# Two transformer blocks on one core: the sandwich norms of the first block taken in two halves of the tokens

## The reference

```python
for l in range(DEPTH):
    h = rms_norm(x, attn_pre_g[l])
    proj = h @ w_in[l]
    ...
    x = x + rms_norm(mixed @ w_out[l], attn_post_g[l])
    h = rms_norm(x, ffn_pre_g[l])
    y = (jax.nn.silu(h @ w_gate[l]) * (h @ w_up[l])) @ w_down[l]
    x = x + rms_norm(y, ffn_post_g[l])
```

## Time and profile before

| | |
|---|---|
| median of 3 runs (lowest to highest) | 2709.44 us (2707.68 to 2710.03) |
| the profiled execution, its own time | 2704.35 us |
| its span, first to last instruction | 2702.6 us |
| TensorE clock granted, share of full | 0.985 |
| PE matmuls busy | 2606.3 us (96%) |
| DVE busy | 1651.4 us (61%) |
| ACT busy | 748.6 us (28%) |
| POOL busy | 456.5 us (17%) |

### The profile page before, as it was taken

How to read it: one execution, slowest core, us unless ns; L and a number is a source line. 1 busy time by engine, 2 the same in 40 slices (tenths; PEclk the granted TensorE clock), 3 DMA queues, 4 the chain that set the end, 5 groups by cost and what they waited for, 6 DMA issues and landing times.

```text
span 2702.6 us, 38398 instructions
## 1 busy us (share of the span) xinstructions
PE 2606.3 (96%) x12250; PEld 2058.9 (76%) x12250; DVE 1651.4 (61%) x2625; ACT 748.6 (28%) x1391; POOL 456.5 (17%) x454
## 2 busy tenths in 40 slices
PE   8999899999899989999899989999999999999999
PEld 5776688887577668888766658888888887788887
DVE  6754666454775566645567776544458888564452
ACT  3333232120333333212145541100025555210000
POOL 4111111112111111212201101111211111112111
PEclk9999999999899999999989999999999999999999
DMA  3221233333122123333312113333332221233333
GB/s 110 55 63 53 76 90 100 94 97 99 48 62 63 55 70 98 96 94 101 93 40 63 54 32 93 101 94 95 99 94 63 63 62 47 78 94 101 93 101 94
DMA packets 417270, 214.80 MB, mean 79 GB/s; under 512 B 6819, under 2 KB 416014, under 8 KB 417166
## 3 DMA queue, kind: packets, MB, share of 16 engines
q1 hardware_dynamic: 416144, 212.89, 27.3%
q10 hardware_dynamic: 1022, 0.58, 0.1%
HBM read 211.34 MB, written 2.10 MB: 79 GB/s over the span
## 4 chain that ended last, share of the span: by engine, by line
PE 84%; DVE 7%; ACT 4%; issue 3%; POOL 1%; DVEq 0%; ACTq 0%; POOLq 0%
PE acc L633 71%; PE sc L740 2%; PE sc L1051 1%; PE tp L633 1%; PE tp L763 1%; PE po L786 1%; PE po L633 1%; ACT scratch L1916 1%; ACT scratch L1914 1%; DVE scratch L1440 1%; PE aux L646 1%; PE tp L902 1%; DVE xT L1359 1%; DVE w_lo L1170 1%; PE po L773 0%
## 5 line engine op out<-in xcount | busy, mean ns | idle before, releaser
L633 PE MATMUL acc<-h_hi,w_hi 128*128 128x512 f32 x1968 | 811.0, 412 | 31.0 <-DVE h_lo L1148 24.4
L576 POOL TENSOR_SCALAR w_hi<-w_raw 128x1024 fp32r<-128x1024 f32 x390 | 418.7, 1074 | 2200.4 <-PE acc L633 2130.3
L633 PE MATMUL acc<-h_lo,w_hi 128*128 128x512 f32 x1968 | 775.0, 394 | 0.0
L633 PE MATMUL acc<-h_hi,w_lo 128*128 128x512 f32 x1968 | 775.0, 394 | 0.0
L1170 DVE TENSOR_TENSOR w_lo<-w_raw,w_hi 128x1024 fp32r<-128x1024 f32 x390 | 477.6, 1225 | 76.3 <-POOL w_hi L576 76.2
L633 PEld LDWEIGHTS acc<-h_hi,w_hi 128*128 128x128 f32 x1968 | 373.2, 190 | 142.6 <-issue 40.4
L633 PE MATMUL acc<-mid_hi,w_hi 128*128 128x512 f32 x1120 | 440.4, 393 | 7.3 <-DVE mid_lo L1701 3.2
L633 PE MATMUL acc<-mid_lo,w_hi 128*128 128x512 f32 x1120 | 440.0, 393 | 0.0
L633 PE MATMUL acc<-mid_hi,w_lo 128*128 128x512 f32 x1120 | 438.2, 391 | 0.0
L633 PEld LDWEIGHTS acc<-h_lo,w_hi 128*128 128x128 f32 x1968 | 373.8, 190 | 80.5 <-issue 10.6
L633 PEld LDWEIGHTS acc<-h_hi,w_lo 128*128 128x128 f32 x1968 | 372.8, 189 | 81.6 <-issue 1.4
(11 more groups left out here) (316 smaller groups left out, 2665.1 us busy)
## 6 DMA issues: line engine op xcount, KB each, us to landing
w_raw<-in_mlp_w_dram SPq DMA_DIRECT2D x128, 512.0 KB, 4.1
w_raw<-in_w_in_dram SPq DMA_DIRECT2D x48, 512.0 KB, 3.9
w_raw<-in_w_gate_dram SPq DMA_DIRECT2D x44, 512.0 KB, 3.7
w_raw<-in_w_up_dram SPq DMA_DIRECT2D x44, 512.0 KB, 3.7
w_raw<-in_w_down_dram SPq DMA_DIRECT2D x32, 512.0 KB, 4.1
w_raw<-in_hg_w_in_dram SPq DMA_DIRECT2D x32, 512.0 KB, 4.0
w_raw<-in_sb_w_qkv_dram SPq DMA_DIRECT2D x24, 512.0 KB, 3.8
w_raw<-in_w_out_dram SPq DMA_DIRECT2D x16, 512.0 KB, 4.1
```

The lines of the kernel that those rows point to most:

```text
L576: nc.gpsimd.tensor_scalar(to, w_raw[:, slot], 1.0, 1.0, ALU.mult, ALU.mult).then_inc(w_rounded, 1)
L633: mm = pe.matmul(bank[:], w[:, k], r[:, k], start=(k == 0 and i == 0), stop=(k == k_tiles - 1 and i == 2))
```

## The change

The 512 tokens are two halves of 256 columns. The last pair of output units is computed half by half (`last_pair`): both units for the first half, then both for the second; the squares of the first half are summed while the second half is multiplied. `normed_update` and `both_norms` scale, update x and form `h_hi` and `h_lo` for the first half of all eight tiles, and then for the second. `side_by_side` runs its units, too, once for each half, each matmul with 256 columns. The first two units now use the extra weight buffers and the other two the main ones, the PSUM banks change accordingly, and the order of the lags is turned round in the second half. The first norm (ahead of the loop) is done in halves with the same functions. The diff, cut:

```diff
-LAGS = [0, 0, 3, 4]
+FIRST_LAGS = [0, 0, 2, 3]
+SECOND_LAGS = [2, 3, 0, 0]
+HALF = S // 2
...
+            round_extra(0)
             for slot in range(2):
-                round_unit(0, slot, w_hi[:, slot], None)
-            round_extra(1)
+                round_unit(1, slot, w_hi[:, slot], None)
...
-                round_units(half + 2, U_GU0 // 2 - 1)
-                round_extra(half + U_GU0 // 2 + 1)
+                round_units(half + 2, U_GU0 // 2 - 2)
+                round_extra(half + U_GU0 // 2)
+                for slot in range(2):
+                    round_unit(half + U_GU0 // 2 + 1, slot, w_hi[:, slot], 2 * half + U_GU0 + slot + 1)
...
+            def sum_half(added, h):
+
+                pe.wait_ge(square_added, added)
+                pe.matmul(aux[:, columns(h)], ones[:, 0:P], square_sum[:, columns(h)], start=True,
+                          stop=True).then_inc(aux_done, 1)
...
+            def last_pair(half, hi, lo, k_tiles, added, a_n, taken):
+
+
+                def of(i, h):
+                    def before(k):
+                        if k == 0 and h == 0:
+                            pe.wait_ge(w_split, 2 * half + i + 3)
+                            pe.wait_ge(evacuated[i], half)
+                        if k == 0 and h == 1:
+                            pe.wait_ge(half_taken, taken + i + 1)
+                    return products(acc[i], hi, lo, w_hi[:, i], w_lo[:, i], k_tiles, unit_done if h else half_done, before,
+                                    columns(h))
+                run(of(0, 0))
+                run(of(1, 0))
+                ops = of(0, 1)
+                run(ops[:14])
+                pe.wait_ge(aux_free, a_n)
+                sum_half(added + KD, 0)
+                run(ops[14:])
+                run(of(1, 1))
+                pe.wait_ge(aux_free, a_n + 1)
...
-            def side_by_side(half, base, n, banks):
-
-                units = [unit(half, i, h_hi, h_lo, ready=h_ready, base=base, fresh=True) for i in range(2)]
-                units += [extra_unit(half + 1, i, bank, base) for i, bank in enumerate(banks)]
-                for k in range(KD + LAGS[len(units) - 1]):
-                    if k in (2, 4, 6, KD - 1):
-                        sum_pair(n * (KD // 2), (k - 1) // 2 if k < KD - 1 else KD // 2 - 1)
-                    for ops, lag in zip(units, LAGS):
-                        if 0 <= k - lag < KD:
-                            run(ops[3 * (k - lag):3 * (k - lag) + 3])
+            def side_by_side(half, norm, banks, added, a_n):
+
+
+                def of(n, h):
+                    def before(k):
+                        if k == 0 and h == 0:
+                            pe.wait_ge(w_split, 2 * half + n + 3)
+                        pe.wait_ge(h_ready, 2 * KD * norm + KD * h + k + 1)
+                    high, low = ((ex_hi, ex_lo) if n < 2 else (w_hi, w_lo))
+                    return products(banks[n], h_hi, h_lo, high[:, n % 2], low[:, n % 2], KD,
+                                    unit_done if h else None, before, columns(h))
+
+                count = len(banks)
+                for h, lags in ((0, FIRST_LAGS), (1, SECOND_LAGS)):
+                    units = [of(n, h) for n in range(count)]
+                    for k in range(KD + max(lags[:count])):
+                        if h == 0 and k == 3:
+                            sum_half(added, 1)
+                        for q, at in enumerate((5, 6, 7, 9) if h == 0 else (3, 4, 6, 7)):
+                            if k == at:
+                                if q == 0:
+                                    pe.wait_ge(aux_free, a_n + h)
+                                sum_pair(norm, h, q)
+                        for n in ((0, 1, 2, 3) if h == 0 else (2, 3, 0, 1)):
+                            if n < count and 0 <= k - lags[n] < KD:
+                                run(units[n][3 * (k - lags[n]):3 * (k - lags[n]) + 3])
...
-                        side_by_side(half0, l * 16, 2 * l, (po, tp[1]))
+                        side_by_side(half0, 2 * l, (sc[0], sc[1], po, tp[1]), added_base(2 * l), A + 1)
...
-                sum_squares(added_base(2 * l), A + AUX["norm_att_post"])
+                last_pair(half0 + U_OUT // 2 + KD // 2 - 1, mid_hi[:, 0], mid_lo[:, 0], KD, added_base(2 * l),
+                          A + AUX["att_post_a"], 4 * l)
...
-                            side_by_side(half, l * 16 + 8, 2 * l + 1, (po, sc[1]))
+                            side_by_side(half, 2 * l + 1, (sc[0], tp[0], po, sc[1]), added_base(2 * l + 1),
+                                         A + AUX["ffn_a"])
...
-                        side_by_side(U_SB // 2, block2_norm(0)[0], 2 * LAYERS, (tp[1],))
-                        work = extra_unit(U_SB // 2 + 1, 1, po, block2_norm(0)[0])
+                        side_by_side(U_SB // 2, 2 * LAYERS, (sc[0], sc[1], tp[1]), added_base(2 * LAYERS), A_SB + 1)
+                        work = products(po, h_hi, h_lo, w_hi[:, 1], w_lo[:, 1], KD, unit_done,
+                                        lambda k: pe.wait_ge(w_split, U_SB + 6) if k == 0 else None)
...
-            v.sem_inc(square_added, 2)
-
-            for j in range(KD):
-                low_part(0, j, gains[:, G_ATT_PRE + j:G_ATT_PRE + j + 1])
-                if j == 0:
-                    split_low(0, 0)
-                    split_low(0, 1)
-                if j % 2:
-                    add_pair(0, 0, j)
-                if j in (4, 6):
-                    split_extra(1, j // 2 - 2)
+            v.memset(square_sum[:, columns(1)], 0.0).then_inc(square_added, 1)
+            v.sem_inc(square_added, 1)
+
+            for h in range(2):
+                for j in range(KD):
+                    low_half(0, h, j, gains[:, G_ATT_PRE + j:G_ATT_PRE + j + 1])
+                    if h == 0 and j == 0:
+                        split_extra(0, 0)
+                        split_extra(0, 1)
+                    if h == 1 and j == 1:
+                        v.wait_ge(aux_done, 1)
+                    if j % 2:
+                        add_pair(KD * h + j + 1, 0, h, j)
+                    if h == 0 and j in (2, 4):
+                        split_low(1, j // 2 - 1)
...
+                def take_half(half, slot, h, n, first):
+
+                    if h == 0:
+                        v.wait_ge(half_done, 2 * n + slot + 1)
+                    else:
+                        take(half, slot)
+                    dst = yT[:, KD - 2 + slot, columns(h)]
+                    done = evacuated[slot] if h else half_taken
+                    if first:
+                        COPY(dst, acc[slot][:, columns(h)]).then_inc(done, 1)
+                    else:
+                        TT(dst, dst, acc[slot][:, columns(h)], ALU.add).then_inc(done, 1)
+
+                def add_half(n, h, slot, before):
+
+                    v.wait_ge(square_ready, squares_base(n) + KD - 2 + (1, 2, 3, 7)[2 * h + slot])
+                    v.wait_ge(square_added, added_base(n) + KD - 2 + before)
+                    s = square_sum[:, columns(h)]
+                    TT(s, s, post_square[slot][:, columns(h)], ALU.add).then_inc(square_added, 1)
+
+                def normed_update(g, n, half, following, first):
+
+                    take_half(half, 0, 0, n, first)
+                    split_extra(following, 0)
+                    add_half(n, 0, 0, 0)
+                    take_half(half, 1, 0, n, first)
+                    add_half(n, 0, 1, 1)
+                    split_extra(following, 1)
+                    take_half(half, 0, 1, n, first)
+                    add_half(n, 1, 0, 2)
+                    norm = n + 1
+                    squares = squares_base(n) + KD - 2
+                    for h in range(2):
+                        c = columns(h)
+                        v.wait_ge(rstd_ready, l * 8 + 2 * g + 3 + h)
+                        for j in range(KD + 1):
+                            if j < KD:
+                                STT(yT[:, j, c], yT[:, j, c], layer_gain[:, g, j:j + 1], rstd[:, c], ALU.mult,
+                                    ALU.mult).then_inc(y_scaled, 1)
+                            if j >= 1:
+                                low_half(norm, h, j - 1, layer_gain[:, g + 1, j - 1:j])
+                                if j % 2 == 0:
+                                    add_pair(squares + (4 + j + KD * h if j > 2 or h else 5), norm, h, j - 1)
+                            if j < KD:
+                                v.wait_ge(y_scaled, 2 * KD * n + KD * h + j + 1)
+                                TT(xT[:, j, c], xT[:, j, c], yT[:, j, c], ALU.add).then_inc(x_ready, 1)
+                            if h == 0 and j == 2:
+                                take_half(half, 1, 1, n, first)
+                                split_low(following + 1, 0)
+                            if h == 0 and j == 3:
+                                add_half(n, 1, 1, 3)
+                            if h == 0 and j == 4:
```

(42 more changed lines are left out.)

161 lines of the change are left out of this document (73 added, 88 removed).

## The result

| | before | after |
|---|---|---|
| median of the runs (lowest to highest) | 2709.74 us (2707.68 to 2711.05) | 2728.31 us (2727.98 to 2732.3) |
| ratio, 95% interval | | 1.0078 [1.0066, 1.009] |
| span of the profiled execution | 2702.6 us | 2730.6 us |

The change makes the kernel slower by 18.6 us, 0.78%. The forecast had the sign and a third of the size: +5.8 us, with a range that ended at 2725. The two profiled spans are 28.0 us apart, more than the medians, since before was profiled 5 us under its median and after 4 us over its own.

The account below looks back on a forecast made before the run. PE, busy 96% of the span, was taken to bound the kernel, with DVE setting the pace inside the stages. The terms -2.4 + 0 + 3.6 + 4.6 gave +5.8 us, a median of 2715.2 us, range 2702 to 2725.

Parts of the forecast that it names:

- DVE sets the pace, not PE: Inside the sandwich stages: DVE, busy 29.73 us of a 38.49 us window in which PE loses 12.2, is the limit.
- Half tile 1.4, 1.7 with a sum: DVE's time per half tile in us, without and with a sum of squares; 24.8 us a stage against 19.6 whole.
- Last `h_lo` ends at L+40.6: Gate/up stage: DVE's last split ends 40.6 us after L, the last output pair's start, 2.0 later than before.
- A gate/up stage gains 1.2: Stage ahead of the gate/up units, in both layers: L+48.2 against L+49.4, so 1.2 us gained, twice.
- Ahead of the second layer: gain 0: Stage between the layers: next work starts at L+47.1 as before, so nothing gained.
- Ahead of the second block 3.6 lost: Stage with three units side by side: next work at L+45.3 against L+41.7, 3.6 us lost.
- The first norm 4.6 lost: Norm ahead of the loop: DVE and PE stop for weight splits, end at 49.2 against 44.55, 4.6 us lost.
- Half a matmul at 0.116: On PE: a 256-column matmul takes 0.116 us, kept within 0.113 to 0.125.
- A: Rival: halves work as drawn, a half costs 0.113 us, clock stays up; 4 us gained, up to 8; chance 0.24.
- B: Rival: nothing to be seen, gains and losses cancel within 5 us; chance 0.13.
- C: Rival: PE's low clock stays through the sparse first halves of four stages, 15 to 25 us lost; chance 0.12.
- D: Rival: weight loads don't hide, a half costs at least 0.20 us, kernel over 2780 us; chance 0.03.

Follow-up runs that it names:

- e5: Changed kernel with e1's edit, and the third ordinary pair put into two PSUM banks the first gate chain has emptied: 2717.23 us, 1.0033.
- e1: Changed kernel with the third ordinary pair's weight split moved into DVE's second gate chain, the next two splits one place earlier: 2726.36 us, 1.0066.
- e6: Changed kernel with the third and fourth unit 4 and 6 tiles behind in first halves (before 2 and 3), first-norm splits later: 2728.69 us, 1.0071.
- e7: Changed kernel without the scaling of y by its factor in the four stages: 2721.34 us, 1.0056.
- e9: Changed kernel with DVE's order altered: y scaled two tiles ahead and x added one tile ahead of h_lo: 2724.58 us, 1.0074.
- e11: Changed kernel with the edits of e3, e5 and e9 together: 2711.74 us, 1.0021.
- e3: Changed kernel with the split of the forget gate's weights issued by DVE directly behind the last half tile: 2727.7 us, 1.0076.
- e4: Kernel before, with the second gate/up chunk's ordinary units run in 256-column matmuls: 2718.53 us, 1.0043.
- e8: Mixture: last output pair, its squares and factor, and y's scaling in halves; everything else whole, including the first norm: 2727.18 us, 1.0073.

## Why the prediction was wrong

By its own steps:

- **"DVE sets the pace, not PE"** failed. The 12.2 us lost in a stage lie ahead of the first tile and in its first few; behind the fourth PE is the slower one, in the trace of before and in the changed kernel. I took DVE's busy 29.73 us for a pace without setting it against PE's 3.17 us a tile. Only ahead of the second block, with three units, does the changed kernel's PE still wait for tiles late in the stage (1.18 us at 1388.48).
- **"Half tile 1.4, 1.7 with a sum"**: measured 1.40 and 1.73. **"Last `h_lo` ends at L+40.6"**: measured 42.96, 44.50, 42.89 and 41.53. DVE's first scaling came at L+12.9, 12.5, 12.6 and 12.1, not 11.4: the split that was to block DVE until L+10.2 ended at L+10.17, but PE's half unit came only then (copy at L+11.0), and an addition met a rounding (0.98 instead of 0.42 us). The rest is more such meetings in the first half (a tile of 3.78 us in the second layer's stage) and waits of DVE for PE's sums (1.21 us, in a tile of 3.04). Only one meeting was in the sum.
- **"A gate/up stage gains 1.2"**: as I cut it, up to the next units, 0.6 was gained, and that it came so near is luck: DVE ended 2.4 us later than forecast, and what follows its end took 5.9 us, not 7.6. But **the cut was the fault**: I let the stage end where PE's next unit starts, and called the rest unchanged. I saw that the first gate unit is done late, "where before a backlog covered it", and charged for it only the 1.4 us of the first split (measured 1.27). The same late end sets off a chain of 17 us, 3.3 us later against L, that before met PE to within 0.4 us. That cost 4.8 us in each layer, and e5 shows that the weights and the bank held by this chain are the cause; it is the largest term that the sum lacks. That the turned lags are what starts it late is read from the traces alone (the chain starts within 0.1 us of the unit's end in the changed kernel, e1, e5, e6, e7, e9 and e11, and 1.6 us behind the factor in all of them).
- **"Ahead of the second layer: gain 0"**: 2.3 lost. DVE's end came late (44.5 for 40.6), and since that stage's pair has six k-tiles its first scaling was at L+13.5 before, not 16.1: there was 1 us to win and not 4.7. The trace of before had it.
- **"Ahead of the second block 3.6 lost"**: 3.64, in part by luck: DVE ended at L+41.5, not 40.3, and what follows took 3.8 us, not 5.0.
- **"The first norm 4.6 lost"**: PE stood still until 23.08 and 26.85 (23.0 and 26.9 forecast) and was done at 49.85 (49.2 forecast): 5.3, by 0.12 us a half instead of 0.116. Behind it came what the sum doesn't have: DVE, busy with halves until 42.07 instead of 29.95, was late with its constants and the forget gate's split (52.57), and with q behind the same constants (e3), 3.8 us more. Together 9.1 us up to L of the first stage, and 7.3 to 9.0 in the other executions of the same code.
- **Half a matmul at 0.116**: 0.1193 in the stages, 0.1200 in e4, inside the bounds of 0.113 to 0.125. On the 288 half matmuls of a stage that is 1 us more than forecast.

Put together for the profiled runs: -1.2 + 2.3 + 3.6 + 5.3 in the windows where I forecast -2.4 + 0 + 3.6 + 4.6, 9.5 behind the gate/up stages and 3.8 behind the norm where I forecast nothing, 0.5 between the layers, 4 by chance.

Of the rivals, A and B are out. C, the low clock, is not what happened: the stages' granted clock was 0.93, 0.90, 0.93 and 0.92, over the same windows before 0.93, 0.85, 0.90 and 0.84, and 16 to 24 of the 226 to 298 half matmuls recorded in a stage took 0.21 us, as at the lower level. D is out by 0.1193. The way it went, a later chain behind the stage, was no rival of mine.

What stays open: the first norm alone was not undone with the rest left in halves, since one loop body of PE serves it and the stage of the second layer; that its loss goes with whole tiles is seen only in e8. Nor was the order of the lags in the second halves turned back, with halves kept, to see the gate chain start earlier.
